# Sparse-expert decoder layer on one core: the first row gather split by expert, one idle product behind the routing, and a tail with other banks, copies and transfers

## What is computed

```python
logits = t @ w_router + b_router              # 4 groups, then 32 experts
# the best group, and in it the best two of its 8 experts; weights e_w
combine = jnp.sum(one_hot(eid, 32) * e_w[..., None], axis=1)
for e in range(32):
    gate, up = jnp.split(t @ w_gate_up[e], 2, axis=-1)    # 1024 -> 2 x 512
    y = (jax.nn.silu(gate) * up) @ w_down[e]              # 512 -> 1024
    out = out + combine[:, e:e + 1] * y
return rms_norm(x + out, final_norm)
```

## Time and profile before

| | us |
|---|---|
| three timed runs | 1242.84, 1243.13, 1246.88 |
| median | 1243.13 |
| the profiled execution's own time | 1247.54 |
| its span in the trace | 1245.8 |
| PE, DVE, ACT, POOL busy in it | 1207.8, 684.6, 389.0, 401.7 |

### The profile page before, as it was taken

How to read it: one execution, slowest core, us unless ns; L and a number is a source line. 1 busy time by engine, 2 the same in 40 slices (tenths; PEclk the granted TensorE clock), 3 DMA queues, 4 the chain that set the end, 5 groups by cost and what they waited for, 6 DMA issues and landing times. The chain is left out here.

```text
span 1245.8 us, 18885 instructions
## 1 busy us (share of the span) xinstructions
PE 1207.8 (97%) x7377; PEld 840.1 (67%) x7377; DVE 684.6 (55%) x1255; ACT 389.0 (31%) x982; POOL 401.7 (32%) x431
## 2 busy tenths in 40 slices
PE   8999999999999999999999999999999999998985
PEld 7788989898888989887687696454453535343432
DVE  2734989999999989763534326532132131212226
ACT  2033745556473736441112133111111111111113
POOL 3266755757574845316331110000000000000011
PEclk9999999999999999999999998999999999999998
DMA  9672221111111212413534246999999999999995
GB/s 358 256 292 80 85 68 53 69 65 71 70 68 52 86 35 85 153 44 130 220 118 152 85 180 260 352 388 427 426 429 427 426 427 427 425 427 428 425 421 229
DMA packets 37304, 287.13 MB, mean 230 GB/s; under 512 B 6524, under 2 KB 6652, under 8 KB 23520
## 3 DMA queue, kind: packets, MB, share of 16 engines
q1 hardware_dynamic: 31488, 273.69, 54.3%
q0 software_dynamic: 3552, 8.20, 1.7%
q10 hardware_dynamic: 2176, 4.03, 0.9%
HBM read 269.84 MB, written 19.92 MB: 233 GB/s over the span
## 5 line engine op out<-in xcount | busy, mean ns | idle before, releaser
L2288 DVE TENSOR_SCALAR ee<-ee 128x256 f32<-128x256 f32 x32 | 9.4, 294 | 308.6 <-ACT ee L2181 308.6
L2265 POOL DMA_INDIRECT expert_out<-yy,row_at x30 | 30.0, 1001 | 414.1 <-ACT yy L2165 403.3
L705 PE MATMUL bank<-h_sums,ring 128*128 128x256 f32 x384 | 92.2, 383 | 0.0
L705 PEld LDWEIGHTS bank<-h_sums,ring 128*128 128x128 f32 x384 | 71.8, 190 | 10.0
L1975 PE MATMUL bank<-one_hot,weights 128*128 128x256 bf16 x448 | 74.1, 273 | 0.0
L1975 PE MATMUL bank<-one_hot,x_rows 128*128 128x256 bf16 x224 | 61.1, 273 | 0.0
L705 PE MATMUL bank<-h_sums,weights_0hi 128*128 128x256 f32 x256 | 60.5, 379 | 0.0
L705 PE MATMUL bank<-h_mix,weights_0lo 128*128 128x256 f32 x256 | 58.7, 382 | 1.4 <-PEq L177 1.4
L715 PE MATMUL bank<-weights_0lo,h_mix 128*128 128x128 f32 x512 | 59.2, 276 | 0.0
L715 PEld LDWEIGHTS bank<-weights_0lo,h_mix 128*128 128x128 f32 x512 | 57.9, 192 | 0.3
L2289 DVE RECIPROCAL ee<-ee 128x256 f32<-128x256 f32 x32 | 56.1, 1752 | 1.1
(11 more groups left out here) (444 smaller groups left out, 2760.0 us busy)
## 6 DMA issues: line engine op xcount, KB each, us to landing
weights_0lo<-in_w_in SPq DMA_DIRECT2D x32, 512.0 KB, 4.2
weights_1down<-in_w_gate_up SPq DMA_DIRECT2D x7, 2048.0 KB, 29.9
weights_0hi<-in_w_gate_up SPq DMA_DIRECT2D x7, 2048.0 KB, 27.8
weights_1hi<-in_w_gate_up SPq DMA_DIRECT2D x7, 2048.0 KB, 35.0
weights_0hi<-in_w_in SPq DMA_DIRECT2D x24, 512.0 KB, 4.0
weights_0lo<-in_w_gate_up SPq DMA_DIRECT2D x6, 2048.0 KB, 25.2
kv_rows<-in_w_gate_up SPq DMA_DIRECT2D x6, 2048.0 KB
weights_1lo<-in_w_gate_up SPq DMA_DIRECT2D x6, 2048.0 KB, 26.1
```

What stands on the lines that cost most here:

```text
L705: mm = pe.matmul(bank[:, 0:HALF_T], w[:, k], h[:, k], start=(fresh and k == 0), stop=(k == HALF_K - 1), skip_group_check=True)
L2265: pool.indirect_dma_start(out=half_rows, out_offset=bass.IndirectOffsetOnAxis(ap=row_at[:, e:e + 1], axis=0), in_=yy[e % 2][:], in_offset= ...
```

## The change

It has five parts. (1) Batch 0 is expert 0 alone, batch 1 expert 1, batch 2 experts 2 and 3; the gather of batch 1 stands behind `hi` of expert 0, that of batch 2 in turn 1. (2) One more idle product, of 512 columns, stands behind the last counting product of the phase before, and `WARM` is 3 rather than 4. (3) DVE splits the rows into bf16 pieces for the four tiles together, after turn 0. (4) The last chunk arrives in two transfers with a semaphore each, and `down` of expert 31 waits for the second half only where it reads it. (5) In the tail, token tiles 2 and 3 exchange their banks, two banks are opened ahead of `down` of expert 30 and one behind the turning of expert 31's hidden rows, ACT makes both copies of expert 31's rows, and the last tile is stored in two halves.

```diff
-BATCHES = 2 + (NE - BATCH) // BATCH
+BATCHES = 3 + (NE - BATCH) // BATCH
...
                 mm = pe.matmul(psum[2][:, 0:NE], g["ones"][:], both[:, u], start=(u == 0), stop=(u == NT - 1))
             mm.then_inc(counts, 1)
+            keep_warm(1)
...
+    if chunk_at(e, part) == 3 * NE - 1:
+        for n, landed in enumerate((g["chunk_landed"][at], g["end_landed"])):
+            columns = slice(n * 2 * D, (n + 1) * 2 * D)
+            eng.dma_start(dst[:, columns], chunk_source(g, e, part)[:, columns]).then_inc(landed, 16)
+        return
...
+FIRST = ((0,), (1,), (2, 3))
 def batch_of(e):
-    return e // 2 if e < BATCH else e // BATCH + 1
+    return min(e, 2) if e < BATCH else e // BATCH + 2
...
-            PAIRS, WARM = NE // 2, 4
+            PAIRS, WARM = NE // 2, 3
...
-                    each = 512 // width
+                    each = min(512 // width, HALF_K)
...
                 def turn(e):
-                    then = 1 if e == 1 else batch_of(e) + 1 if e % BATCH == BATCH - 1 and e < NE - 1 else None
+                    then = e + 1 if e < 2 else batch_of(e) + 1 if e % BATCH == BATCH - 1 and e < NE - 1 else None
...
-                    if then:
+                    if then and e:
                         gather_half(then, 0)
                     pe.wait_ge(x_taken, KC * batch_of(e) + KC)
                     chunk_in(pe, g, e, "hi")
                     gate_up(pe, column, buffer_of(g, e, "hi"), U[q], range(HALF_K, KC)).then_inc(gu_mm, 1)
+                    if then and not e:
+                        gather_half(then, 0)
                     if then:
                         gather_half(then, 1)
...
+                    if e == NE - 1:
+                        pe.wait_ge(hid_got, NE - 1)
+                        open_bank(pe, 0)
+                        open_bank(pe, 6)
                     if e:
                         down_of(e - 1, 1 - q)
...
+                hidden_of(NE - 1, 1)
                 pe.wait_ge(late_got, LATE)
-                pe.wait_ge(hid_got, NE - 1)
-                open_bank(pe, 0)
-                open_bank(pe, 1)
-                open_bank(pe, 6).then_inc(opened, 1)
-                hidden_of(NE - 1, 1)
+                open_bank(pe, 1).then_inc(opened, 1)
                 open_bank(pe, 2)
                 open_bank(pe, 3)
...
-                dve.wait_ge(gathered, fills_before(1))
-                dve.wait_ge(gu_lo_mm, 1)
                 for e in range(NE):
-                    if e == 0:
-                        split_rows(0, 0)
                     turn(e)
                     if e == 0:
-                        for t in range(1, NT):
+                        dve.wait_ge(gathered, fills_before(2))
+                        dve.wait_ge(gu_lo_mm, 1)
+                        for t in range(NT):
                             split_rows(t, 0)
...
-        return [psum[2 * t + n] for n in range(2)]
+        return [psum[2 * (0, 1, 3, 2)[t] + n] for n in range(2)]
...
-    def last_rows(dve):
...
-            if t == 1:
-                last_rows(dve)
-            if t < 3:
-                dve.wait_ge(v["opened"], t + 1)
+            dve.wait_ge(v["opened"], (1, 2, 2, 3)[t])
...
     def sync_last(sp):
+            if t < NT - 1:
+                sp.wait_ge(done, t + 1)
+                sp.dma_start(rows, y2[:, t]).then_inc(stored, 16)
+                continue
+            for n in range(2):
+                half = slice(n * 512, (n + 1) * 512)
+                sp.wait_ge(done, NT + n)
+                sp.dma_start(rows[:, half], y2[:, t, half]).then_inc(stored, 16)
```

More of the change, by code:

```diff
@@ L1895, in load_over @@
     eng.dma_start(dst, chunk_source(g, e, part)).then_inc(g["chunk_landed"][at], 16)
+FIRST = ((0,), (1,), (2, 3))
 def batch_of(e):
-    return e // 2 if e < BATCH else e // BATCH + 1
+    return min(e, 2) if e < BATCH else e // BATCH + 2
 def experts_of(b):
-    return range(2 * b, 2 * b + 2) if b < 2 else range(BATCH * (b - 1), BATCH * b)
+    return FIRST[b] if b < 3 else range(BATCH * (b - 2), BATCH * (b - 1))
 def fills_before(b):
-    return 2 * b if b < 2 else 4 * (b - 1)
-FILLS = 4 * (BATCHES - 1)
+    return 2 * b if b < 3 else 6 + 4 * (b - 3)
+FILLS = fills_before(BATCHES)
 def expert_phase(nc, psum, g):
@@ L1998, in down @@
                 half, c = divmod(f, 2)
+                if swapped and f == FC // 2:
+                    pe.wait_ge(g["end_landed"], 16)
                 for n in range(2):
@@ L2052, in gather_half @@
                         pe.wait_ge(picked, b + 1)
[L2053 removed]
+                    if b == 3:
                         pe.wait_ge(split, 3 * NT * (upper + 1))
@@ L2156, in rows_out @@
                         rows, others = slice(q * SLOTS, (q + 1) * SLOTS), slice((1 - q) * SLOTS, (2 - q) * SLOTS)
-                        if e == NE - 1:
-                            act.activation(late_yy[0][rows, :], Y[q][rows, :], ACT.Copy).then_inc(y_got, 1)
-                            return
                         act.activation(late_yy[0][rows, :], Y[q][rows, :], ACT.Copy).then_inc(late_got, 1)
@@ L2181, in turn @@
                     act.activation(ee[q][:], U[q][:, 0:FF // 2], ACT.Exp, scale=-1.0).then_inc(ex, 1)
+                    if then and not e:
+                        take_half(then, 0)
                     if then:
@@ L2270, in choose @@
                 def choose(b):
-                    if b > 1:
+                    if b > 3:
                         dve.wait_ge(gathered, fills_before(b))
@@ L2275, in choose @@
                         for t in range(NT):
-                            mark = dve.tensor_scalar((sel if b < 2 else one_hot)[:, t, column:column + SLOTS], g["slot_row"][:],
+                            mark = dve.tensor_scalar((sel if b < 3 else one_hot)[:, t, column:column + SLOTS], g["slot_row"][:],
                                                      R["at_slot"][:, t, e:e + 1], None, ALU.is_equal)
@@ L2322, in late_choice @@
                     last_one.then_inc(maxrow, 1)
-                choose(0)
-                choose(1)
+                for b in range(len(FIRST)):
+                    choose(b)
                 row_table(dve)
-                dve.wait_ge(gathered, fills_before(1))
-                dve.wait_ge(gu_lo_mm, 1)
                 for e in range(NE):
-                    if e == 0:
-                        split_rows(0, 0)
                     turn(e)
                     if e == 0:
-                        for t in range(1, NT):
+                        dve.wait_ge(gathered, fills_before(2))
+                        dve.wait_ge(gu_lo_mm, 1)
+                        for t in range(NT):
                             split_rows(t, 0)
@@ L2535, in sync_last @@
         for t in range(NT):
-            sp.wait_ge(done, t + 1)
-            sp.dma_start(g["out"][0].rearrange("(n p) d -> n p d", p=P)[t], y2[:, t]).then_inc(stored, 16)
-        sp.wait_ge(stored, 16 * NT)
+            rows = g["out"][0].rearrange("(n p) d -> n p d", p=P)[t]
+            if t < NT - 1:
[6 more added lines that the diff above has]
+                sp.dma_start(rows[:, half], y2[:, t, half]).then_inc(stored, 16)
+        sp.wait_ge(stored, 16 * (NT + 1))
     def tensor_last(pe):
@@ L2597, in vector_last @@
                 half = slice(n * 512, (n + 1) * 512)
-                last = dve.scalar_tensor_tensor(y2[:, t, half], bank[:], rf[:, c], final_g[:, half], ALU.mult, ALU.mult)
-            last.then_inc(done, 1)
+                scaled = dve.scalar_tensor_tensor(y2[:, t, half], bank[:], rf[:, c], final_g[:, half], ALU.mult, ALU.mult)
+                if n or t == NT - 1:
+                    scaled.then_inc(done, 1)
     def scalar_last(act):
```

9 lines of the change are left out of this document (3 added, 6 removed).

## The result

The changed kernel takes 1249.59 us (median of 7 runs, 1249.29 to 1252.24), the kernel before 1245.52 (7 runs, 1242.84 to 1248.08). The ratio is 1.0037, 95% interval 1.0024 to 1.0051: slower, by 4.1 us in the medians. The time lies in the forecast range, but the forecast called "no change" likelier than "slower". The profiled execution of the changed kernel took 1250.84, with a span of 1249.1.

The account below looks back on a forecast made before the run. PE's work before the tenth load was taken to set the weight stream's end: +2.65 there, -2.2 and -0.6 in the tail gave -0.15, or 1247.4 us; less 1.3 for the median's scale, 1246.1, range 1241.3 to 1249.7.

Parts of the forecast that it names:

- The rival of the early start: Phase's first weight load sets the stream's end, so its earlier issue shows: some 1239.6 us; chance 0.04.
- The sum for the profiled pair: Whole change against the profiled execution: 2.65 - 2.2 - 0.6 = -0.15 us, from 1247.54 to 1247.4.
- the front: PE's work up to the tenth load: -2.1 - 1.7 + 6.6 - 0.15 = +2.65 us.
- For 64 columns I take 0.103: Spacing of gather instructions on PE: 64 take 6.6 us per expert, bounds 6.5 to 7.1.
- The rival that columns count: 64-column gather instructions take 0.056 us, each gather 3.6: 6 us less in all, 1240.1; chance 0.08.
- the tail, forecast at -2.8: End of the kernel: 2.2 us less on DVE and 0.6 less from the last tile in halves.
- Its 2.2 on DVE: DVE's sums in the tail lose the 0.68 copy and 1.55 bank wait: 2.2 us less.
- the condition that I had put on this term: DVE's 2.2 us gain in the tail holds if the later pairs of gathered rows land in time.
- the last tile in halves: Only half of 512 KB is left to move behind the last scaling: 0.6 us less at 427 GB/s.
- That the tail gives nothing: Rival: late row pairs or PE's half clock take the tail's gain: 1246.1 + 2.8 = 1248.9 us; chance 0.10.
- the 2.1: At the seam the idle product keeps PE at 2.4 GHz, so the gather starts at 761.1, 2.1 us earlier.
- My sum without the half clock, +3.0: Taking 1.3 us off 1247.4 to reach the median's scale gives 1246.1, 3.0 above the median of before.

Follow-up runs that it names:

- the two kernels with 17 idle products: Kernel before plus 17 idle products of 256 columns, behind `hi` of expert 2 (1250.89 us) or in turn 10 (1244.94 us); before 1245.45.
- seam and tail: Changed kernel without the split of the first gather, seam and tail as changed: 1243.23 us, ratio 0.9987 to the kernel before.
- the tail alone: Kernel before with only the changed tail (banks, copies, halves of last chunk and last tile): 1243.46 us, ratio 0.9987.
- The seam alone: Kernel before with one idle product behind the counting products and three instead of four behind the seam: 1244.44 us, ratio 0.9991.
- the kernel with the down product moved ahead: Changed seam and tail, no split, down product ahead of the gather's second half in turns with a gather: 1241.3 us, second series 1242.97.
- the kernel with idle products in turn 10: Kernel before with 17 idle products of 256 columns behind the upper half of expert 10: 1244.94 us, ratio 0.9996.

## Why the forecast was right and wrong

**Right: what bounds the kernel.** PE up to the tenth load sets the end. The break stood where it was expected (832 to 834 us, load at 833.96), the early first load bought nothing, and the two kernels with 17 idle products showed both sides of it. From the tenth load to the landing of expert 31's upper half it is 377.6 to 378.7 in all nine kernels in which the last break stands at the tenth load. The rival of the early start falls. That the moved splitting of the rows costs nothing was right too: the first gather from pieces follows at 816.17 without a wait.

**The steps that failed are two terms of the sum.** The sum for the profiled pair was -0.15, and measured is +3.3 (1249.1 - 1245.8). Of what it lacks the front has 1.2, the tail 2.0 and the stream between them 0.25. That the time lies in the range all the same is luck: it does so by 0.1 (1249.59, with an upper end of 1249.7), and the upper end had been set for rivals that are not what happened.

**The first: the gathers.** "For 64 columns I take 0.103": measured are 7.09 and 7.29 for 64, which is 0.111 and 0.114 each. This is at and just above the upper bound that I had named, from the row of 128 columns. The row of 36 columns, 0.102, misled: it is a group of 8, while the groups of 64 instructions, of 64 or 128 columns, give 0.111 to 0.115. The two gathers took 14.4 and not 13.2, and the front came to +3.89 and not +2.65. The rival that columns count falls altogether. The rule of the Trainium skill, "TensorE: Matmul & The Clock Gate", section "LDWEIGHTS (loading the stationary operand)", gives a load of 128 columns 128 / 1.2 GHz, or 107 ns, and the moving columns don't enter. By it the estimate for two gathers is 13.6, nearer to the measured 14.4 than my 13.2. The trace agrees in that 64 columns cost what 128 do, and lies a little above in size (0.111 to 0.114).

**The second, and larger: the tail, forecast at -2.8, gave -0.8 in the profiled pair.** Its 2.2 on DVE are there: the last sum ends 2.0 earlier, counted from the landing of expert 31's upper half (25.09 behind it, 27.10 before). But the 2.2 held a wait of 1.55 that was half the doing of PE's half clock, since it is 0.70 at full clock. In the changed kernel PE's products and ACT's squares then took 1.15 back (4.84 against 3.69); in seam and tail, and in the tail alone, they did not. There DVE's wait for the rows of tile 1 took 0.49 and 0.70, which is the condition that I had put on this term, and DVE's first sum began 14.9 and 14.4 behind the landing of expert 31's upper half where it was 14.2 before. And the last tile in halves gave nothing: from the end of the last scaling to the end of the span it is 3.1 in both (1242.74 to 1245.8, 1246.02 to 1249.1). Tile 2's store, issued only 1.3 ahead of the last half (1244.73 and 1246.05), still has bytes to move: the transfer engines are busy without a break from 1245.5 to 1248.2. I had counted the last tile's bytes alone. That the tail gives nothing, a rival with 0.10, came nearest to what happened there.

**The clock at the seam.** In the profiled execution it held, 1.00 as forecast, and the 2.1 came out (761.13). But as a mechanism the step is not borne out: it fell behind the idle product in other kernels, and held without it. The seam alone is worth 1.2 in the medians, with an interval that reaches to nothing.

**The scale.** I took the median of before, 1243.13, for an execution without the half clock, and took 1.3 off. Three series of 29, 25 and 21 further runs of before have medians of 1245.62, 1245.45 and 1245.25, and its shortest run of all is 1242.84: the first three runs had given a value near the bottom of its spread. Between the shortest runs the change costs 6.45 (1249.29 - 1242.84). My sum without the half clock, +3.0, with the two corrections (+1.3 for gathers of 7.19 instead of 6.6 beside 7.14 for the old one, +2.0 in the tail) is 6.3, close to the 6.45; with a tail that gives nothing at full clock, as the table has it, it is 7.1. Between the medians it is 4.1, because before's median holds part of a half clock, and the changed kernel's does in fewer runs. The mean granted clocks of the timed runs bear it out in part. In before's three series the 18 runs at 0.998 or more have a median of 1243.5 and the 28 runs at 0.995 or less one of 1247.3. The changed kernel has 1249.31 in its 3 runs at 0.998, so at like clock the change costs 5.8, and 1250.84 to 1252.24 in its 3 runs at 0.995 and 0.996. That this is the reason for the whole difference of 2.3 is not shown: these means don't say where the clock was low.

**Left open.** Why PE's clock falls at the seam in some executions and not in others. Why ACT's copy in the tail started 1.8 behind the modelled end of the product that it reads (1228.18 against 1226.35); before, the copy that followed that product was 0.95 behind. Over the 12 profiled executions it is 0.95 to 1.83 in five (before, changed kernel, seam alone, tail alone, seam and tail), in all of which PE's first pair of the tail ran at half clock in whole or in part, and 0.04 to 0.06 in the other seven, in one of which it did. No run was made on either.

## What to carry to other kernels

Splitting a gather by products to start earlier costs the full count of stationary blocks again, and here 64 moving columns were no cheaper than 128; it pays only if the load that it brings forward is the last that the stream waits for. Find that load by the last break in the bandwidth, and price only what stands ahead of it. A wait that shrinks when another engine runs at its full clock is no fixed gain, and three runs are too few where more than one execution in three has another clock level somewhere.

## What was unexpected of the hardware

- A float32 product instruction with a 128x128 stationary block came every 0.111 to 0.115 us in groups of 64, with 64 moving columns (7.09 and 7.29) as with 128 (7.14 and 7.33).
- PE's granted clock at the same seam of nearly the same program was 0.50 to 0.59 in 5 of 12 profiled executions and 1.00 in 7; with work of the same kind ahead of it both times. In the tail it was 0.50 behind a pause of 3.2 us in the changed kernel, and in the second series of the kernel with the down product moved ahead it was 1.00 behind one of 3.09. The same pause of 3.11, in the seam alone and in the kernel with idle products in turn 10, came out both ways:

```profile
1222.20 1.10 PE L2566 MATMUL bank<-ring 128*128 128x512 f32 x2 [3.09 <-DVE bank L2586]
1223.13 1.02 PE L2566 MATMUL bank<-yy,ring 128*128 128x512 f32 x2
```

```profile
1224.59 2.07 PE L2551 MATMUL bank<-ring 128*128 128x512 f32 x2 [3.11 <-DVE yy L2565]
```

```profile
1223.53 1.13 PE L2553 MATMUL bank<-ring 128*128 128x512 f32 x2 [3.11 <-DVE yy L2567]
```
